# A two-layer decoder trunk on one core: the second layer's first projection tile in front of its gate section, and the gate products in two halves around the transposes

## What is computed

```python
for i in range(DEPTH):                                   # DEPTH = 2
    mod = jax.nn.silu(c) @ ada_w[i] + ada_b[i]
    sh_a, sc_a, g_a, sh_f, sc_f, g_f = jnp.split(mod[:, None, :], 6, axis=-1)
    h = rmsnorm(x, norm_mix[i]) * (1.0 + sc_a) + sh_a
    y = diff_attention(h, ...) if i % 2 == 0 else retention(h, ...)
    x = x + g_a * y
    h = rmsnorm(x, norm_ffn[i]) * (1.0 + sc_f) + sh_f
    x = x + g_f * moe(h, ...)                            # 64 experts, 8 per token, and a shared one
return rmsnorm(x, final_norm)
```

## Time and profile before

| | us |
|---|---|
| median of 3 runs | 1422.04 |
| lowest and highest of the runs | 1421.65, 1423.11 |
| the profiled execution, its own time | 1421.86 |
| its span, first to last instruction | 1420.1 |

### The profile page before, as it was taken

How to read it: one execution, slowest core, us unless ns; L and a number is a source line. 1 busy time by engine, 2 the same in 40 slices (tenths; PEclk the granted TensorE clock), 3 DMA queues, 4 the chain that set the end, 5 groups by cost and what they waited for, 6 DMA issues and landing times.

```text
span 1420.1 us, 33005 instructions
## 1 busy us (share of the span) xinstructions
PE 1323.9 (93%) x12029; PEld 871.4 (61%) x12030; DVE 550.3 (39%) x1226; ACT 448.8 (32%) x891; POOL 220.3 (16%) x684
## 2 busy tenths in 40 slices
PE   4899889999999999899699999899999999999996
PEld 2888675555455555445499998765555555555553
DVE  2565683333233232222543355653332323322334
ACT  3444542222122222112444454522222222222222
POOL 8200102111111111111200000021111111111110
PEclk9999999999999999999899999999999999999999
DMA  9998978999999999999995435659999999999995
GB/s 353 338 356 319 405 299 342 420 422 422 422 421 423 422 422 421 423 422 421 371 331 181 149 121 176 234 227 422 420 422 422 422 422 422 421 422 422 422 421 214
DMA packets 113978, 516.07 MB, mean 363 GB/s; under 512 B 10280, under 2 KB 47264, under 8 KB 64000
## 3 DMA queue, kind: packets, MB, share of 16 engines
q1 hardware_dynamic: 109920, 509.64, 89.6%
q0 software_dynamic: 3296, 3.50, 0.9%
q10 hardware_dynamic: 704, 2.10, 0.4%
HBM read 514.11 MB, written 1.09 MB: 363 GB/s over the span
## 4 chain that ended last, share of the span: by engine, by line
PE 66%; DMA 11%; SPq 8%; DVE 6%; ACT 5%; issue 3%; ACTq 1%; DVEq 0%
PE bank L966 17%; PE bank L1148 15%; PE bank L1169 7%; PE bank L1151 7%; PE bank L1083 6%; DMA ring<-in_exp_w_dram 6%; PE bank L1124 5%; SPq L352 3%; PE bank L1175 3%; SPq L346 3%; DMA mods<-in_exp_w_dram 2%; PE bank L941 2%; DMA ring<-in_da_w_in_dram 2%; SPq L355 2%; DMA ring<-in_ret_w_in_dram 1%
## 5 line engine op out<-in xcount | busy, mean ns | idle before, releaser
L1148 PE MATMUL bank<-ring,arena 128*64 128x512 f32 x768 | 178.6, 605 | 9.9 <-DMA ring<-in_exp_w_dram 9.9
L1124 PEld LDWEIGHTS bank<-arena 128*128 128x128 bf16 x3264 | 142.1, 98 | 55.5 <-issue 55.0
L1083 PE MATMUL bank<-arena_r 128*128 128x512 f32 x560 | 161.2, 418 | 3.0 <-DVE arena_r L1621 3.0
L1621 DVE TENSOR_TENSOR arena_r<-bank,arena_r 128x512 fp32r<-128x512 f32 x136 | 94.1, 692 | 154.1 <-ACT arena_r L747 154.1
L1124 PE MATMUL bank<-arena 128*128 128x64 bf16 (+1 forms) x3264 | 151.8, 207 | 0.0
L740 ACT ACTIVATE arena<-bank 128x256 f32<-128x256 f32 (+1 forms) x68 | 22.6, 333 | 387.4 <-PE bank L1148 270.1
L554 POOL TENSOR_TENSOR arena<-arena,pass_base 128x2 f32 x136 | 24.7, 205 | 743.2 <-PE bank L1135 729.2
L747 ACT CAST arena_r<-bank 128x512 fp32r<-128x512 f32 x136 | 79.7, 586 | 189.4 <-PE bank L1169 124.8
L1083 PEld LDWEIGHTS bank<-arena_r 128*128 128x128 f32 x560 | 94.6, 188 | 60.2 <-issue 47.5
L966 PE MATMUL bank<-HH_r,ring_r 128*128 128x256 f32 x448 | 127.7, 285 | 0.0
L1148 PEld LDWEIGHTS bank<-ring,arena 128*64 128x64 f32 x768 | 56.5, 139 | 111.4 <-issue 110.8
(11 more groups left out here) (277 smaller groups left out, 2163.8 us busy)
## 6 DMA issues: line engine op xcount, KB each, us to landing
ring<-in_exp_w_dram SPq DMA_DIRECT2D x264, 1024.0 KB, 24.0
ring<-in_ada_w_dram SPq DMA_DIRECT2D x48, 1024.0 KB, 12.3
HH<-in_exp_w_dram SPq DMA_DIRECT2D x40, 1024.0 KB, 21.0
mods<-in_exp_w_dram SPq DMA_DIRECT2D x40, 1024.0 KB, 25.0
arena<-in_exp_w_dram SPq DMA_DIRECT2D x40, 1024.0 KB, 25.0
ring<-in_ret_w_in_dram SPq DMA_DIRECT2D x24, 1024.0 KB, 11.8
ring<-in_da_w_in_dram SPq DMA_DIRECT2D x12, 1024.0 KB, 15.3
ring<-in_ret_w_out_dram SPq DMA_DIRECT2D x8, 1024.0 KB, 4.9
```

Of the source, the lines that this page charges most:

```text
L1083: ins = nc.tensor.matmul(banks[4 + NH * tc + hf][:, :], S[:, P * tc:P * tc + P], y[:, r, 512 * hf:512 * hf + 512], start=False, stop=(last ...
L1124: ins = nc.tensor.matmul(banks[2 - 2 * half][:, P * kk:P * kk + 2 * W], parts[:, tc, r, P * (4 * half + kk):P * (4 * half + kk + 1)], Pg[: ...
L1148: ins = nc.tensor.matmul(banks[1][W * i:W * i + W, :], xg[:, k, W * i:W * i + W], w13[j][:, k, :, :], start=(k == 0), stop=(k == KD - 1))
L1621: nc.vector.tensor_tensor(y[:, 1, 512 * hf:512 * hf + 512], banks[hf][:, :], y[:, 0, 512 * hf:512 * hf + 512], ALU.subtract).then_inc(u[f" ...
```

## The change

The first projection tile of layer 1 stands ahead of the four gate tiles in the stream. PE makes the gate section's products for the first four slices, then the transposes, then the other four slices, and only then the projection. The gate section goes to bank 4 instead of bank 3, so its first product waits until DVE has read banks 4 and 5 (`x_new` 3), and the transposes no longer wait until ACT has read that bank. ACT copies the section out behind the rounding of tile 1 instead of between the two norms, and releases its four slots after the eviction of projection tile 0. The projection's banks are turned by two places, and its tile 2, the first to use bank 4, waits for that copy.

```diff
--- before.py
+++ after.py
@@ -51,7 +51,7 @@
     order += [("shared", 0, i) for i in range(3)] + [("pad",)]
     moe = {0: len(order)}
     order += [("expert", 0, i) for i in range(132)]
-    order += later[8] + [("mix_in", 1, i) for i in range(24)] + [("mix_out", 1, i) for i in range(8)] + later[9]
+    order += [("mix_in", 1, 0)] + later[8] + [("mix_in", 1, i) for i in range(1, 24)] + [("mix_out", 1, i) for i in range(8)] + later[9]
     order += [("shared", 1, i) for i in range(3)] + [("pad",)]
     moe[1] = len(order)
     order += [("expert", 1, i) for i in range(132)]
@@ -313,9 +313,9 @@
                 turns.append(("ada", BESIDE[i]))
         turns += [("ada", k) for k in range(4, 7)]
         proj0_bank = {i: banks[7 * (n % 2)] for n, (kind, i) in enumerate(turns) if kind == "proj"}
-        proj1_bank = {i: banks[3 + ((i + 1) % 4 if i < 16 else (i + 1) % 2)] for i in range(24)}
+        proj1_bank = {i: banks[3 + ((i + 3) % 4 if i < 16 else (i + 1) % 2)] for i in range(24)}
         ada_bank = {k: banks[7 * (n % 2)] for n, (kind, k) in enumerate(turns) if kind == "ada"}
-        ada_bank.update({7: banks[4], 8: banks[3], 9: banks[4]})
+        ada_bank.update({7: banks[4], 8: banks[4], 9: banks[4]})
 
         split = [("mix_in", 0, i) for i in range(12)] + [("mix_out", 0, i) for i in range(4)] + [("shared", 0, i) for i in range(2)]
         split += [("mix_in", 1, i) for i in range(24)] + [("mix_out", 1, i) for i in range(8)] + [("shared", 1, i) for i in range(2)]
@@ -620,10 +620,6 @@
                         act.wait_ge(eps_set, 1)
                     act.wait_ge(sumsq, TC * n + tc + 1)
                     nc.scalar.activation(rs[:, tc:tc + 1], ss[:, tc:tc + 1], ACT.Sqrt, scale=1.0 / D, bias=eps[:, 0:1]).then_inc(root, 1)
-                    if n == 2 and tc == 0:
-                        act.wait_ge(ada_done, 2 + 8 + 1)
-                        nc.scalar.copy(raw2_1, ada_bank[8][:, 0:256]).then_inc(bank_rows_read, 1)
-                        release(4)
                 norms[0] += 1
 
             def evict_hT():
@@ -863,9 +859,13 @@
             norm_stats()
             evict_hT()
             round_w("mix_in", 1, 1)
+            act.wait_ge(ada_done, 2 + 8 + 1)
+            nc.scalar.copy(raw2_1, ada_bank[8][:, 0:256]).then_inc(bank_rows_read, 1)
             def evict_proj1(i):
                 if i < 4:
                     evict_proj(qT[:, 2 * i:2 * i + 2, :])
+                    if i == 0:
+                        release(4)
                 elif i < 8:
                     if i == 4:
                         act.wait_ge(rows_stored, 320)
@@ -932,16 +932,17 @@
 
         @block.tensor
         def _(pe):
-            def ada(l, s, bank):
+            def ada(l, s, bank, ks=range(KD)):
                 tiles = [where["ada", l, 4 * s + q] for q in range(4)]
-                for k in range(KD):
+                for k in ks:
                     if k % 2 == 0:
                         arrived(pe, tiles[k // 2])
                     for q in range(4):
                         ins = nc.tensor.matmul(bank[32 * q:32 * q + 32, :],
                                                cb[:, k, :], tile_out(tiles[k // 2])[:, k % 2, 256 * q:256 * q + 256],
                                                start=(k == 0), stop=(k == KD - 1))
-                ins.then_inc(ada_done, 1)
+                if k == KD - 1:
+                    ins.then_inc(ada_done, 1)
 
             norms = [0]
 
@@ -1316,10 +1317,13 @@
             moe(0)
 
 
-            ada(*LATER[8], ada_bank[8][:, 0:256])
-            pe.wait_ge(bank_rows_read, 9)
+            pe.wait_ge(x_new, 3)
+            ada(*LATER[8], ada_bank[8][:, 0:256], range(KD // 2))
             turn_h()
+            ada(*LATER[8], ada_bank[8][:, 0:256], range(KD // 2, KD))
             for i in range(16):
+                if i == 2:
+                    pe.wait_ge(bank_rows_read, 9)
                 project(1, i, token_major=(i >= 8))
 
             def gate_half(j, m):
```

## The result

| | before | after |
|---|---|---|
| runs of the comparison | 1422.57 us, median of 4 (1421.65 to 1424.55) | 1411.76 us, median of 4 (1411.42 to 1412.00) |
| ratio | | 0.9922, 95% interval 0.9901 to 0.9943 |
| profiled execution, span | 1421.86, 1420.1 | 1411.42, 1409.7 |
| granted TensorE clock, mean of the span | 0.982 | 0.988 |

The kernel is faster, by 10.8 us, and the interval says 8.1 to 14.1.

What follows compares the result with a forecast made beforehand. Experts were taken to go at the loads' pace; at layer 1's border everything waited for the projection's first tile. 1421.86 - 8.5 = 1413.3, plus 0.2 for the median and 0.2 for the clock: 1413.7 us, range 1412.3 to 1416.0.

Steps and rivals of the forecast that it cites:

- The wait: Layer 1's border: with the projection's first tile moved up, the norm starts at the residual rows, saving 8.5 us.
- a change of kinds: Load stream: landings 4.5 us apart where the kind of tile changes, against 2.57 for a gate tile, 3.0 for a projection tile.
- The section's halves: Gate section's products on TensorE: both halves cost nothing, with 0.8 us of cover left to the first projection product.
- The fourth gate tile: Last tile of the gate section, now fifth in the queue: lands at 694.0 at the latest, needed only at 695.4.
- The third rival: Fourth gate tile late: each us after 696.9 costs one, slower than before from 705.4; chance 0.02.
- The ring and the copy: Projection slots and ACT's section copy: SP not held, eighth tile at 706; copy has 17 us of cover, costs nothing.
- given back: Second rival: layer 1's experts wait for loads that start no earlier, so the 8.5 us are lost, 1422; chance 0.04.
- The clock at the border: TensorE's thin work from 687.9 to 697.1: a clock fall is likely, costing nothing to 2.5 us, taken as 0.2.
- the 1415 to 1416: First rival: clock falls in the thin stretch and stays low in the projection, costing 1 to 2.5 us; chance 0.12.
- How the numbers follow: Chances and range of the whole time: 1412.3 to 1416.0, down by 1.5 us of run scatter, up by 2.5 of clock.
- The sum: Whole kernel: the profiled execution's 1421.86 less 8.5 is 1413.3; 1413.5 for the median, 1413.7 with the clock.

Runs made afterwards that it cites:

- e5: Changed kernel with the fourth gate tile one place later in the stream, behind projection tile 1: 1413.95 us, ratio 0.9950 to the kernel before.
- e2: Changed kernel with the whole gate section in one piece ahead of the transposes: 1417.34 us, ratio 0.9964 to the kernel before.
- e3: Changed kernel with the whole gate section in one piece behind the transposes: 1414.98 us, ratio 0.9948 to the kernel before.
- e9: Changed kernel with the fourth gate tile three places later in the stream, behind projection tile 3: 1422.65 us, ratio 0.9999 to the kernel before.
- r1_after: Changed kernel run again without any edit, on the third chip: 1412.22 us against 1421.19 for the kernel before, ratio 0.9941.
- r4_before: Kernel before run again without any edit, on the third chip, for a third profile: 1422.21 us in a single run.
- e6: Kernel before with 60 idle transposes added behind the gate section: 1472.23 us, ratio 1.0358 to the kernel before.
- e10: Kernel before with 30 idle transposes added behind the gate section: 1424.57 us in one run.
- e7: Changed kernel with 20 idle transposes added behind the row transposes ahead of either MoE: 1425.50 us, median of 12 runs.
- e1: Kernel before with the new stream order alone, gate slots released behind tile 0's eviction: 1419.28 us, ratio 0.9981 to the kernel before.

## Why the prediction was right in its steps and low in its gain

**The wait.** "The difference is 8.5 us": 8.54 at the border, 8.5 in every one of the four profiles of the changed kernel against the three of before. The tile landed at 681.3 (its queue time was 15.6 us; I had it at 682.3 to 683.8), the rounding ran at 682.24, h stood 2.89 us behind X where I took 2.90 from the norm of MoE 1, and the first product at 3.85 us behind h, released by DVE as forecast. One reading was wrong and cost nothing: I had put 4.5 us between two landings down to a change of kinds, but in the changed kernel the projection's tile lands 2.9 us behind the last expert tile, and it is the fourth gate tile that lands 4.3 us behind the third (675.8 + 13.2 = 689.0).

**The section's halves.** Costed at nothing, and they cost nothing: 0.84 us of cover were left to the first product, 0.8 predicted. e5 shows that 1.6 us more of lateness are absorbed, e2 and e3 that either whole form pays 2.1 and 2.4 us.

**The fourth gate tile.** The working had it "needed only at 695.4"; it landed at 693.3. The long issue was not that of the projection's tile, which took 0.58 us, but that of the first gate tile, 8.0 us; the queue was deep enough for that too. In e9 the price ran past one for one: 12.5 us after X is 6.0 past the point given (6.5 after X), and the time rose by 7.7 us at the products' start and 1.0 in them, since the standing still also let the clock fall. The third rival's point from which the kernel is slower than before, 705.4 with X at 690.38 or 15.0 after X, was therefore too late: at 12.5 us after X the gain was already gone.

**The ring and the copy.** SP's issue of the eighth projection tile, at 705.2 where I had 706, and POOL's store changed nothing: from the products' start to the mixer's end both kernels take 203.5 us. The loads of MoE 1 start earlier with the rest, so nothing was given back (480.43 and 480.13 us for its experts).

**The clock at the border.** The sum had 0.2 us for it. In three of four profiles it did not fall, in r1_after it fell and was covered. The kernel before is no better off: in r4_before the clock was low among the products (92.64 instead of 91.41). The Trainium skill, "TensorE: Matmul & The Clock Gate", section "Part 1: The HAM clock gate", says that the throttled clock comes back after TensorE has been idle. The trace of e3, with its stop of 5.60 us and its clock of 0.55, agrees. The changed kernel's own thin stretch stayed at 1.00 in three of four profiles, so the 1415 to 1416 that the prediction had by that rule did not come.

**The step that failed.** It is "How the numbers follow", its sentence on the range: "down by the scatter of the runs (1421.65 to 1423.11, 1.5 us)", and with it the base in "The sum", one execution's own time. Three runs of before within 1.5 us were taken for the scatter of the kernel. The 76 runs of the kernel before in these comparisons spread from 1418.80 to 1426.06, and the 16 of the changed one from 1410.88 to 1417.02: 6 to 7 us. The term that I had given no size at all is what the stretches that the change does not touch differ by from one execution to the next: 3.7 us to X between two executions of the changed kernel and 0.9 ahead of MoE 1, in company with the granted clock. The profiled execution should have taken 1421.86 - 8.54 = 1413.3 and took 1411.42; the missing 1.9 us are these stretches. That the four runs of the comparison all fell near the lower end of the spread was luck. That the range missed was not luck alone: of the 16 runs of the changed kernel nine lie under 1412.3. Over all runs the means are 1422.11 and 1413.42, 8.7 us apart, the medians 1422.00 and 1412.19, 9.8 apart; 8.5 us lie inside all three intervals (8.1 to 14.1, 6.4 to 10.5, 5.8 to 9.2).

**What stays open.** Whether the changed kernel has a further gain of its own of up to an us: the medians allow it. The stretch ahead of MoE 1 took 23.05 to 23.14 us in all three profiles of before and 22.24 to 22.39 in three of the four of the changed kernel, with the clock of that window at 0.89 and 0.94. Against a gain of its own speaks that both levels occur with either order of the stream: 0.94 also in e6 and e10, which are the kernel before with idle transposes, and 0.89 also in e2 and e9, which have the new order. But the changed kernel may shift the fall more often to where it costs less, and seven profiles cannot tell. What sets where the clock falls in layer 0 in one execution and not in the next was not found, nor was it shown that the stops in e6 and e7 are the loading of code; an experiment that only moves the code was not made. No version ran clearly faster than the changed kernel.

## What to carry to other kernels

When the chain shows a long transfer in front of an in-order engine whose real inputs are there already, price the change by the next waiter: here the nearest same norm elsewhere in the trace gave 2.90 us against 2.89 measured. Moving a tile up and leaving the work behind it alone only renames the wait (e1). What is pushed down the queue must get its new place in the programs too, first of all where an in-order engine picks up its result between two steps of the chain (5.0 us here), and three tiles in front of it eat the whole gain (e9). Before giving a range of 0.1% take the scatter from many runs and compare stretches cut at events, not totals.

## What the runs showed of the chip that I had not expected

- Two executions of one kernel differ by up to 6 to 7 us of 1415, and in the changed kernel the time goes with the mean granted clock (0.983 to 0.989). Whether a fall costs anything depends on where it comes: from 350 to 370 nothing, from 655 to 670 1.0 to 1.9 us, ahead of MoE 1 0.1 to 1.2.
- Behind a stop of 5.60 us at the border (e3) the clock was 0.55; 6.77 us of idle transposes ahead of a stop of 2.98 us (e6) did not keep it up, and it was 0.68 and then 0.50 from 700 to 710.
- 60 more instructions in one place gave eight stops of 4 to 6 us in the expert loop of layer 1, with 81 instead of 44 packets on the instruction queue; 30 gave none.
- One issue of a 1 MB load held SP for 8.0 us, in the changed kernel and in e9, and so set when the tiles behind it went out.
